# Latent attention: sums of squares in three pieces, and a pair's head units ahead of the ZC products

## The reference, cut to what matters

```python
q = (rms_norm(c_q, q_a_g) @ w_uq).reshape(B, L, MLA_HEADS, QK_DIM)
kv = (rms_norm(c_kv, kv_a_g) @ w_ukv).reshape(B, L, MLA_HEADS, NOPE_DIM + V_DIM)
k_nope, v = kv[..., :NOPE_DIM], kv[..., NOPE_DIM:]
k = jnp.concatenate([k_nope, k_r], axis=-1)
q = rms_norm(q, q_norm_g)
k = rms_norm(k, k_norm_g)
...
o = causal_block_attention(q, k, v)
return o.reshape(B, L, MLA_HEADS * V_DIM) @ w_proj
```

## Time and profile before

| | |
|---|---|
| median of 3 runs | 2772.9 us (2770.89 to 2774.07) |
| the profiled execution | 2774.93 us |
| its span | 2773.2 us |
| mean granted TensorE clock | 0.97 of 2.4 GHz |
| TensorE busy | 2652.4 us (96%) |
| VectorE, ScalarE, GpSimd busy | 1578.3, 1083.2, 984.7 us |

### The profile page before, as it was taken

The page is one execution under the profiler, slowest core; times in us unless marked ns, Lnnn a source line. Parts: engine busy times, 40 slices in busy tenths (PEclk is TensorE's granted clock), DMA queues, the critical chain, the costliest instruction groups (busy, mean ns, idle before and its releaser), DMA issues.

```text
span 2773.2 us, 43947 instructions
## 1 busy us (share of the span) xinstructions
PE 2652.4 (96%) x16728; PEld 2345.4 (85%) x16728; DVE 1578.3 (57%) x2426; ACT 1083.2 (39%) x1800; POOL 984.7 (36%) x492
## 2 busy tenths in 40 slices
PE   7998999999899998999999999999999999999998
PEld 5787678888689998888999999989987777788887
DVE  5665523224489886443366664598884343566642
ACT  4445423223432433342344543323324342454432
POOL 2111344444334222111455544443221113565554
PEclk9998999999899999989999999999999899999999
DMA  4220232323222111101322221232111012332223
GB/s 152 65 85 24 69 108 91 98 91 97 71 69 91 61 54 58 37 31 39 120 87 96 103 92 62 90 92 77 54 54 56 31 39 69 122 107 92 92 69 114
DMA packets 61757, 215.27 MB, mean 78 GB/s; under 512 B 8144, under 2 KB 8144, under 8 KB 61584
## 3 DMA queue, kind: packets, MB, share of 16 engines
q1 hardware_dynamic: 49280, 173.63, 19.3%
q10 hardware_dynamic: 11936, 37.99, 4.1%
q0 software_dynamic: 368, 1.23, 0.1%
HBM read 210.65 MB, written 2.16 MB: 77 GB/s over the span
## 4 chain that ended last, share of the span: by engine, by line
PE 50%; issue 26%; POOLq 13%; DVE 5%; POOL 3%; DVEq 2%; ACT 1%; DMA 0%; ACTq 0%
POOLq L605 12%; PE ps L691 12%; PE ps L692 12%; PE ps L693 12%; POOL dl L618 3%; PE ps L1121 2%; PE ps L674 2%; PE ps L972 1%; PE ps L1096 1%; PE ps L914 1%; PE ps L915 1%; PE ps L916 1%; DVE arena L1931 1%; PE ps L1112 1%; DVEq L2448 1%
## 5 line engine op out<-in xcount | busy, mean ns | idle before, releaser
L604 POOL TENSOR_TENSOR wl<-stage,wh 128x1024 fp32r<-128x1024 f32 x326 | 792.4, 2431 | 1699.5 <-ACT wh L1259 1697.3
L691 PE MATMUL ps<-Uh,wh 128*128 128x264 f32 (+1 forms) x2640 | 896.8, 340 | 27.7 <-DVE Ul L1937 10.4
L692 PE MATMUL ps<-Ul,wh 128*128 128x264 f32 (+1 forms) x2640 | 867.4, 329 | 0.0
L693 PE MATMUL ps<-Uh,wl 128*128 128x264 f32 (+1 forms) x2640 | 864.7, 328 | 0.0
L1259 ACT ACTIVATE wh<-stage 128x1024 fp32r<-128x1024 f32 x326 | 345.4, 1060 | 1059.7 <-PE ps L693 1056.8
L691 PEld LDWEIGHTS ps<-Uh,wh 128*128 128x128 f32 x2640 | 505.9, 192 | 90.3 <-issue 13.3
L693 PEld LDWEIGHTS ps<-Uh,wl 128*128 128x128 f32 x2640 | 504.7, 191 | 42.7
L692 PEld LDWEIGHTS ps<-Ul,wh 128*128 128x128 f32 x2640 | 506.4, 192 | 39.9 <-issue 2.4
L2529 DVE SCALAR_TENSOR_TENSOR ps<-arena,v,ps 128x528 f32<-128x528 f32 x232 | 167.9, 769 | 8.3
L692 PE MATMUL ps<-HIDl,wh 128*128 128x512 f32 (+1 forms) x448 | 162.8, 363 | 0.0
L693 PE MATMUL ps<-HIDh,wl 128*128 128x512 f32 (+1 forms) x448 | 162.1, 362 | 0.0
(11 more groups left out here) (366 smaller groups left out, 4811.7 us busy)
## 6 DMA issues: line engine op xcount, KB each, us to landing
stage<-w SPq DMA_DIRECT2D x326, 512.0 KB, 3.5
dstage<-w_down ACTq DMA_DIRECT2D x48, 512.0 KB, 4.3
arena<-bias_rows ACTq DMA_DIRECT2D x16, 448.0 KB, 5.5
arena<-w_mla ACTq DMA_DIRECT2D x8, 384.0 KB, 2.9
H<-xT SPq DMA_DIRECT2D x8, 256.0 KB, 6.5
out<-H ACTq DMA_DIRECT2D x8, 256.0 KB, 2.8
arena<-pT SPq DMA_DIRECT2D x1, 512.0 KB, 7.8
arena<-causal POOLq DMA_DIRECT2D x1, 320.0 KB, 3.1
```

The lines of the kernel that those rows point to most:

```text
L604: pool.tensor_tensor(wl[:, j, :], stage[:, j, :], wh[:, j, :].bitcast(F32), ALU.subtract).then_inc(w_split, 1)
L691: pe.matmul(dst, w_lead, tok.part(a_lead, h), start=(k == 0), stop=False)
L692: pe.matmul(dst, w_lead, tok.part(a_rest, h), start=False, stop=False)
L693: mm = pe.matmul(dst, w_rest, tok.part(a_lead, h), start=False, stop=(k == len(acts) - 1))
```

## The change

`head_sums` on TensorE becomes a generator of three steps (first head's squares, second head's, keys'), and its one wait for three squares becomes two waits, for one and for two more. `sums_beside` puts the three pieces between the product steps of another unit: piece, product step, piece, product step, piece, and then the rest of the unit. That unit is the gate unit in set-up and the first ZC unit in pairs 0 to 2. The head units of pair p + 1 stand ahead of the first ZC unit now. The steps of a pair after the change: 1 to 8 gate 1; 9 and 10 first queries; 11 keys; 12 and 13 second queries; 14 values; 15 the first piece; 16 to 19 the first ZC unit, with the second piece in step 16 and the third in step 17; 20 to 23 the second ZC unit; 24 on as before. On ScalarE the squares and copies move with them (first queries from step 14 to 10, keys from 15 to 11, second queries from 17 to 13, values from 18 to 14, roots from 19 to 17). On VectorE the rotations move from steps 14 and 17 to 10 and 13, the inverses from 21 to 19, and the first ZC unit's `branch` from 12 to 19, behind the inverses. Pair 3 keeps its order. The number of steps and of instructions is the same.

```diff
--- before.py
+++ after.py
@@ -84,6 +84,7 @@
 FILL_LEVEL = 3
 FILL_KEYS, FILL_UPDATE, FILL_OUTPUT, FILL_SUMS, FILL_SPREAD, FILL_LAST = 3, 2, 4, 4, 3, 1
 LATENT_SETUP = 18
+SUM_STEPS = 3
 FILL_BEFORE, FILL_BESIDE, FILL_BEHIND = (2, 2), (2, 1), (1, 2)
 
 
@@ -1130,18 +1131,28 @@
                     b = at["unit"] % 2
                     at["unit"] += 1
                     pe.wait_ge(unit_free[b], n.next(unit_free[b]))
-                    pe.wait_ge(qk_raw, n.next(qk_raw, 3))
                     for hd in range(2):
+                        pe.wait_ge(qk_raw, n.next(qk_raw, (1, 2)[hd]))
                         for i in range(QT):
                             rows = P if i < QT - 1 else META
                             pe.matmul(ps[0:rows, 2 * b, hd * QT + i:hd * QT + i + 1], relu[0:QK, hd, i * P:i * P + rows],
                                       ones[0:QK, 0:1], start=True, stop=True)
+                        yield
                     pe.matmul(ps[0:T2.rows, 2 * b + 1, 0:2 * T2_TILES], ident[0:T2.rows, 0:T2.rows], ropess[0:T2.rows, :],
                               start=True, stop=False)
                     for i in range(T2_TILES):
                         mm = pe.matmul(ps[0:T2.rows, 2 * b + 1, 2 * i:2 * i + 2], ksq[:, i * T2.rows:(i + 1) * T2.rows],
                                        halves, start=False, stop=(i == T2_TILES - 1))
                     mm.then_inc(unit_done[b], 1)
+                    yield
+
+                def sums_beside(unit):
+                    parts = head_sums()
+                    next(parts)
+                    yield
+                    for k in unit:
+                        next(parts, None)
+                        yield
 
                 def key_scales():
 
@@ -1168,23 +1179,22 @@
                     yield from unit_steps([tile(pair, 2), tile(pair, 3)], [cq[:, 0, :], cq[:, 1, :]], T2)
                     values(pair)
                     yield
-                    head_sums()
-                    yield
 
                 def latent_units():
 
                     yield from unit_steps([fold[NOPE:P, :]], [kraw[NOPE:P]], T2)
                     yield from head_units(0)
-                    yield from split_steps(split_chunk(), U2k, kept)
+                    yield from sums_beside(split_steps(split_chunk(), U2k, kept))
                     yield from key_scales()
                     for pair in range(4):
                         yield from split_steps(split_chunk(), U2k, kept)
+                        if pair < 3:
+                            yield from head_units(pair + 1)
                         tiles = split_chunk()
                         if pair == 0:
                             pe.wait_ge(zc_ready, n.next(zc_ready, HEADS_G))
-                        yield from split_steps(tiles[0:4], ZCk, kept)
-                        if pair < 3:
-                            yield from head_units(pair + 1)
+                        first = split_steps(tiles[0:4], ZCk, kept)
+                        yield from sums_beside(first) if pair < 3 else first
                         yield from split_steps(tiles[4:8], ZCk, kept)
                         if pair < 3:
                             yield from key_scales()
@@ -1827,6 +1837,7 @@
                     yield
                     copy_vt(pair)
                     yield
+                    yield from idle(SUM_STEPS - 1)
                     head_roots()
                     yield
 
@@ -1834,8 +1845,8 @@
                     pass_units(2)
                     yield from idle(2)
 
-                def gate_unit(j):
-                    yield from idle(KD - 1)
+                def gate_unit(j, steps=KD):
+                    yield from idle(steps - 1)
                     gate(j)
                     yield
 
@@ -1843,15 +1854,14 @@
                     rope_keys()
                     yield
                     yield from head_units(0)
-                    yield from gate_unit(0)
+                    yield from gate_unit(0, KD + 1 - SUM_STEPS)
                     yield from key_scales()
                     for pair in range(4):
                         yield from gate_unit(1)
-                        take()
-                        yield from idle(4)
                         if pair < 3:
                             yield from head_units(pair + 1)
-                        yield from idle(3)
+                        take()
+                        yield from idle(5 if pair < 3 else 7)
                         used_up()
                         yield
                         if pair < 3:
@@ -2761,7 +2771,7 @@
                     for _ in range(count):
                         yield
 
-                def head_units():
+                def head_units(beside=None):
                     yield from idle(1)
                     turned_queries(0)
                     yield
@@ -2770,7 +2780,11 @@
                     turned_queries(1)
                     yield
                     pass_units(2)
-                    yield from idle(2)
+                    yield from idle(2 + SUM_STEPS)
+                    head_inverses()
+                    if beside is not None:
+                        beside()
+                    yield
 
                 def key_scales():
                     for hd in range(2):
@@ -2782,22 +2796,18 @@
                     yield
                     yield from head_units()
                     take()
-                    yield from idle(2)
-                    head_inverses()
-                    yield from idle(KD - 2)
+                    yield from idle(KD - 1 - SUM_STEPS)
                     yield from key_scales()
                     for pair in range(4):
                         take()
-                        yield from idle(KD + 3)
-                        branch(2 * pair, 0, False)
-                        yield
+                        yield from idle(KD)
                         if pair < 3:
-                            yield from head_units()
-                            yield from idle(1)
-                            head_inverses()
-                            yield from idle(2)
+                            yield from head_units(lambda: branch(2 * pair, 0, False))
                         else:
                             yield from idle(3)
+                            branch(2 * pair, 0, False)
+                            yield
+                        yield from idle(3)
                         branch(2 * pair + 1, 1, False)
                         yield
                         if pair < 3:
```

## The result

The change makes the kernel slower. The median of 4 runs is 2803.9 us (2802.1 to 2807.1) against 2772.7 us for the kernel before (4 runs, 2770.9 to 2774.1); the ratio is 1.0115, 95% interval 1.0102 to 1.0127. Forecast were +35 us, measured are +31. The profiled execution took 2807.1 us, 32.2 more than the one of before.

What follows compares the result with a forecast made beforehand. TensorE, busy for 96% of the span, was taken as the bound. Waits of +21.6 us, clock +14.5 and set-up -1 gave +35 us on the profiled 2774.9, less 2 for the median: 2808 us, range 2790 to 2825.

Steps and rivals of the forecast that it cites:

- The order costs a wait: In six pairs, head units moved ahead make TensorE wait at the values and second queries: 3.6 us each, +21.6 us.
- the walk: Pair 1 of layer 1, followed through the engines' queues: late masking delays raw keys, so the values wait 3.3 us.
- The clock's term: In six pairs, low clock begins at the wait, 15.5 us each: 93 us against 57, +14.5 us.
- The split as a gain: Sums in three pieces can by themselves only win clock: at most 23 us in pairs and 2.7 us in set-up.
- The price of low time: In the latent stretches, each microsecond at 1.2 GHz costs 0.4 us, taken from pairs doing the same work.
- Set-up: In set-up there is no new wait and the pieces alone act: -1 us (0 to -2.7).
- A: Rival: the wait alone, with the clock low about as long as now: +21.6 us, 2794 us; chance 0.20.
- B: Rival: the clock stays low through both heads, 22 us a pair: 2824 us; chance 0.10.
- C: Rival: the clock holds in spite of the wait: 2770 to 2778 us, no change; chance 0.03.
- D: Rival: ScalarE frees the keys' bank in time and the split gives its clock back: faster, 2750 us; chance 0.05.

Runs made afterwards that it cites:

- Keys first: Changed kernel with ScalarE's raw-keys step taken ahead of a pair's last two exponentials: 2791.9 us.
- move alone: Kernel before with only the head units moved ahead of the first ZC unit, sums in one piece: 2795.2 us, again 2800.2 us.
- wide sums: Kernel before with each sum matmul reading the column of ones 96 times: 2759.8 us; 128 times: 2759.2 us; 32 times: 2774.0 us.
- split alone: Changed kernel with head units back behind the first ZC unit, sum pieces between the second ZC unit's products: 2780.8 us.

## Why the prediction was right, step by step

**The order costs a wait.** Right in place and cause, and nearly in number. Predicted was a wait of 3.3 us at the values and 0.8 in place of 0.4 at the second queries, 3.6 us a pair in all; measured are 2.99 us, and 0.59 in place of 0.18, so 3.4 us of idle time, and by pairs of equal clock 3.8 us (the 46.0 and 49.8 above; 48.7 and 52.5) to 4.6 (51.7 and 56.3). The chain of square, rotation, masking, maxima, exponentials and raw keys is the one of the walk; the masking is 2.1 us late (predicted 2.15). Keys first takes the wait away. The 0.5 us or so above the idle time are not in my sum: I had taken the longer steps as moved work only. In layer 2's pair 0.4 us of it is time in which TensorE is busy (48.34 us against 47.92, with as many matmuls but for one). Six pairs: 23 to 25 us against 21.6.

**The clock's term.** Right in sign, too large. Predicted were 36 us more at 1.2 GHz in the six pairs and +14.5 us. By the two profiles' clock the six pairs have 55 us low before and 68 after, 14 more, or 11 us a pair where I had taken 15.5. The two windows with the six pairs, before and then after:

```profile
1117.10:1269.10 152.00, 149.93 (x991) 128.75 (x992) 64.42 (x147) 58.34 (x128) 19.89 (x8) 0.90 0.11 35
2121.90:2268.90 147.00, 144.87 (x775) 109.78 (x776) 64.06 (x147) 58.27 (x128) 19.85 (x8) 0.92 0.11 36
...
1114.40:1281.90 167.50, 154.91 (x991) 133.16 (x992) 64.00 (x147) 57.96 (x128) 19.82 (x8) 0.89 0.10 32
2138.20:2300.00 161.80, 149.32 (x774) 114.12 (x775) 63.79 (x147) 57.80 (x128) 19.75 (x8) 0.91 0.10 32
```

With the pairs' starts to the hundredth they are 30.5 us longer; 23 to 25 are the order, and 5 to 7 are left, which agrees with 14 x 0.4. Over whole executions the changed kernel has 10 to 33 us more at the lower level than before.

The place was right in part: I wrote that the low stretch begins at the wait and not at the sums. In the profile after it begins ahead of the first piece in three of six pairs, 0 to 1.7 us behind the end of the wait, and 5.4 to 5.8 us behind it, behind the second piece, in the others, as in layer 1's pair 0, where the clock was 1.00 through the wait and the first two pieces (1131.8 to 1140.2) and 0.50 behind them (1140.2 to 1150.4).

So the fall at the wait is real, but it replaced the fall at the sums more than it was added to it: the move alone, with the same wait and the same place of the fall in four pairs, has 0 to 5 us more low time than before. On top of it the split costs clock (8 us of time and 27 us low against the move alone in the same set). Where wide sums had taken the old fall away, the wait does add: 168 us low with it, 134 and 142 without.

**The split as a gain.** I had said that by itself it can only win clock. That step failed: the split alone has 185 us low against 167, and costs 7 us. The runs show that; they don't show why. One reading is that the sums and the product steps between them, two for three pieces, make one longer stretch in which the array reads little, so that the upper level is given back later. That the same sums with 96 columns bring it down to 134 us speaks for it; but 10 us are left above the 124 of wide sums in one piece, and it isn't shown beyond that.

**The price of low time.** Taken as 0.4 us each from pairs of before, and right. Wide sums against before beside them: 13.5 us for 43 us low, and 13.8 for 46. That looks like 0.3, but the slower pace of the wide sums has to be added, 3.5 and 4.7 us: 0.4 both times. The split alone gives 7.4 us for 18, 0.4 again. The Trainium skill (TensorE: Matmul & The Clock Gate, HAM oscillation) counts half of the throttled time. The measured price is lower here. The prediction says that waits absorb the difference; no run shows that.

**Set-up.** Predicted -1 us. The profile has -1.5 in layer 1 and +4.3 in layer 2, where the clock of the stretch is 0.76 (above). The move alone, whose set-up is that of before, has +2.7 there: so most of it isn't the split of the sums in set-up. The sign was wrong, by some 4 us of the sum.

**Rivals.** A (the wait alone, 2794) is nearest to the move alone, and B's 22 us of low clock a pair didn't come. C and D needed the wait to be short or the clock to hold: neither did (the stretches have 0.91 and 0.90, in layer 2 less than the 0.93 of before). C's own sum, 21.6 - 23 - 2, is -3.4, which is 2769.5 and not in its 2770 to 2778; and D's 2772.9 - 23 - 2.7 is 2747 and not 2750; neither makes a difference here. With 23 to 25 for the order, 5 to 7 for the clock in the pairs and 3 for set-up, the sum is 33 for 32 measured between the two profiled executions; the medians have 31.

**How much of it was luck.** The total came out closer (35 against 31) than its terms. The clock was put some 8 us too high, the order 1 to 3 and set-up 4 too low, and these errors cancel in part. The order alone carries the direction.

## What to carry to other kernels

When a group of steps is moved in a hand-written order, walk each engine's queue at the new place: one short operation that waits (here a rotation of 0.7 us, for a square behind an exponential) delayed a masking by 2 us, and the bank that was freed at the end of that chain was the one TensorE wanted next. With units that alternate between two banks, ask of every unit who frees its bank and what stands ahead of that in its queue. Matmuls with one moving column took 0.11 us each here, and 32 columns hardly more (2.37 us for 2.25). Giving them 96 or 128 columns to read kept the clock up at a small cost of pace (0.4 to 0.6 us for twenty), and it did more (-14 us) than putting product steps between them (+7 us). Before a price for low time is taken from such a run, what the edit itself costs has to be added.

## What was not expected of the hardware

- Matmuls with weights of 96 x 128 and one moving column (0.11 us each) let the granted clock fall although TensorE was busy throughout; with 96 or 128 moving columns, at 0.13 and 0.14 us each, time at 1.2 GHz fell from 163 to 167 us to 117 to 124 us per execution, with 32 columns it didn't (159).
- Breaking a stretch of such matmuls up with product steps of 0.75 us raised the time at 1.2 GHz (167 to 185 us), where I had expected less of it.
- A wait of 3.0 us ahead of TensorE, six times, moved the fall of the clock forward to its end (four of six pairs of the move alone), but left the time at 1.2 GHz about as it was (168 us against 167 and 163). With wide sums the same wait added to it (168 us against 134 and 142), and once it left a whole pair at 1.00.
- The profiled executions of the changed kernel, from two sets of runs, both have 56.9 us for layer 2's pair 1 and 52.6 and 52.4 us for pairs 0 and 2: the order in which the clock falls repeats from run to run more than I had thought.
